# A fused two-layer transformer kernel on one core: five more landing places for expert weights, first weight parts run on the first 128 tokens, query rests moved to VectorE

## The reference, cut to what matters

```python
def peer_ffn(h, w_q, sub_keys, expert_u, expert_v):
    ...
        q = (hb @ w_q).reshape(PEER_TOKEN_BLOCK, PEER_HEADS, 2, PEER_HALF)
        s = jnp.einsum('thpc,hpkc->thpk', q, sub_keys).astype(jnp.float32)
        top_s, top_i = lax.top_k(s, PEER_TOPK)
        ...
        u = expert_u[idx]
        act = jax.nn.gelu(jnp.einsum('thkd,td->thk', u, hb).astype(jnp.float32), approximate=False)
        wts = (gates * act).astype(hb.dtype)
        return jnp.einsum('thk,thkd->td', wts, expert_v[idx])

def hybrid_layer(x, c, lb, rel_bias, ...):
    ...
    (aq, ak, av, iq, ik, iw, bq, bf, bi, bg, cq, ck, cv, cg, ga, gb, gc) = split_cols(h @ w_in)
    ...
    x = x + gt1 * (merged @ w_out)
    h2 = rmsnorm_2(x, norm2_g) * (1.0 + sc2) + sh2
    x = x + gt2 * hier_moe(h2, rg_w, rg_b, re_w, re_b, e_gate, e_up, e_down)
    return x
```

## Time and profile before

| | us |
|---|---|
| median of 3 runs (lowest, highest) | 2014.12 (2011.47, 2016.54) |
| the profiled execution, its own time | 2012.58 |
| its span in the trace | 2010.8 |

### The profile page before, as it was taken

One profiled execution on the slowest core, in us unless ns is written; L12 is line 12 of the kernel. 1 busy time (PEld: TensorE's weight loads), 2 busy tenths in 40 slices (PEclk: granted clock), 3 DMA queues, 4 the chain that ended last, 5 costly groups with the idle time before them and its releaser, 6 DMA issues.

```text
span 2010.8 us, 21920 instructions
## 1 busy us (share of the span) xinstructions
PE 1658.6 (82%) x8644; PEld 1020.0 (51%) x8644; DVE 988.1 (49%) x1894; ACT 547.6 (27%) x951; POOL 616.4 (31%) x396
## 2 busy tenths in 40 slices
PE   7998977677777777777999998999999867676765
PEld 7784942232222223236999988987884311111211
DVE  6462666876778775553663886554434100000001
ACT  4342421212222212123453544445622000000001
POOL 3431643444444444433674105443320000000000
PEclk9999998999999999998999999999999877778878
DMA  8755499999999999984544433554586999999997
GB/s 336 302 200 217 191 374 421 422 420 421 421 421 421 418 419 414 419 366 149 171 165 159 147 106 126 187 186 156 184 348 248 422 421 422 421 421 421 421 422 319
DMA packets 92228, 634.73 MB, mean 316 GB/s; under 512 B 10940, under 2 KB 13628, under 8 KB 16472
## 3 DMA queue, kind: packets, MB, share of 16 engines
q1 hardware_dynamic: 50832, 353.39, 45.1%
q0 software_dynamic: 36864, 268.45, 32.4%
q10 hardware_dynamic: 4424, 11.42, 1.6%
HBM read 632.15 MB, written 1.08 MB: 315 GB/s over the span
## 4 chain that ended last, share of the span: by engine, by line
PE 47%; DMA 42%; DVE 7%; ACT 2%; issue 2%; POOL 0%; SPq 0%; DVEq 0%; ACTq 0%
DMA t<-in_expert_uv,t 21%; PE ps L555 6%; PE ps L557 6%; PE ps L560 6%; DMA t<-in_eg 6%; DMA ring<-in_ed 5%; DMA t<-in_ed 5%; PE ps L596 3%; PE ps L755 3%; DMA ring<-in_eg 3%; PE ps L609 3%; PE ps L758 3%; DVE t L2018 3%; PE ps L575 2%; PE ps L576 2%; PE ps L581 2%
## 5 line engine op out<-in xcount | busy, mean ns | idle before, releaser
L179 POOL TENSOR_TENSOR t<-ring,t 128x1024 fp32r<-128x1024 f32 x125 | 320.8, 2576 | 474.7 <-ACT t L171 474.4
L755 PE MATMUL ps<-t 128*128 128x512 f32 x496 | 275.6, 638 | 163.3 <-ACT t L1384 163.2
L2685 POOL DMA_INDIRECT t<-in_expert_uv,t x248 | 280.9, 1133 | 360.3 <-PE ps L758 340.1
L2018 DVE CUSTOM_DVE_ANT_0 t<-t 128x1024 f32<-128x1024 f32 x248 | 303.0, 1226 | 171.9 <-DMA t<-in_expert_uv,t 169.4
L171 ACT ACTIVATE t<-ring 128x1024 fp32r<-128x1024 f32 x220 | 230.6, 1054 | 238.8 <-PE ps L560 87.2
L758 PE MATMUL ps<-t 128*128 128x512 f32 x496 | 260.0, 606 | 0.0
L755 PEld LDWEIGHTS ps<-t 128*128 128x128 f32 x496 | 87.3, 195 | 326.1 <-ACT t L1384 261.8
L1057 PE MATMUL ps<-t 128*32 128x512 f32 x864 | 144.5, 765 | 74.6 <-DMA t<-in_eg 28.0
L179 DVE TENSOR_TENSOR t<-ring,t 128x1024 fp32r<-128x1024 f32 x95 | 129.2, 1366 | 134.9 <-ACT t L171 132.1
L555 PE MATMUL ps<-t 128*128 128x256 f32 x1120 | 164.7, 291 | 15.1 <-ACT t L171 5.5
L1377 ACT ACTIVATE t<-t 128x2 f32<-128x2 f32 x129 | 26.2, 203 | 507.9 <-DVE t L2018 507.5
(11 more groups left out here) (358 smaller groups left out, 1841.5 us busy)
## 6 DMA issues: line engine op xcount, KB each, us to landing
ring<-in_w_in SPq DMA_DIRECT2D x82, 1024.0 KB, 5.0
t<-in_eu SPq DMA_DIRECT2D x38, 1024.0 KB, 26.9
t<-in_eg SPq DMA_DIRECT2D x36, 1024.0 KB, 26.9
t<-in_ed SPq DMA_DIRECT2D x34, 1024.0 KB, 27.3
ring<-in_ed SPq DMA_DIRECT2D x30, 1024.0 KB, 27.0
ring<-in_eg SPq DMA_DIRECT2D x28, 1024.0 KB, 26.8
ring<-in_eu SPq DMA_DIRECT2D x26, 1024.0 KB, 27.1
ring<-in_ada_w SPq DMA_DIRECT2D x20, 1024.0 KB, 7.5
```

The costliest lines, as they stand in the source:

```text
L179: e.tensor_tensor(p.lo, p.view, p.hi.bitcast(F32), ALU.subtract).then_inc(self.w.lo[eng], 1)
L755: ins = e.matmul(sums[tt][0], s.diag[col % 4], v[:, 1024:1536], start=first, stop=last)
L2018: ins = e.tensor_tensor_reduce(out=g[:, 0:1024], in0=g[:, 0:1024], in1=s.hN[:, col // 128, :], scale=1.0, scalar=0.0, op0=ALU.mult, op1=AL ...
L2685: m.gathered[s.place[col]].up(e.indirect_dma_start(out=s.gb[col], out_offset=None, in_=m.a_in["expert_uv"], in_offset=bass.IndirectOffsetO ...
```

## The change

**Expert places.** The ring `m.s4.w` has 18 places, and a 19th stands alone as `m.s4.w0` and holds the first `eg` chunk. The new ones are `more`, `g12` (rows 1 and 2 of `grow`, now in one tensor), `hT`, `x` and `selT`; `rw` and `cm` move into `sgb`. SP loads `more` and `selT` when the last `w_branch_c` matmul is done (`mc4`, 3, 3), now ahead of the two first ring buffers; then the ring as before; then `g12` after the last of four `h3` steps, `hT` after the router's matmuls (`route`), `x` after the matmuls that read it (`x_read`), and only then goes on with the places of `ada_w_2`. A branch for overfull experts (not taken with these inputs) turns the activations anew.

**First parts.** `pe_cols_begun` runs a part's 24 matmuls over the first 128 tokens as soon as tile 0 is there; `pe_cols` then does the other 128. It is used for 1 part in stage 1, 3 in stage 2 and 4 in stage 3.

**Rests.** Six of the 13 `w_q` rests of GpSimd (p7, p8, p9, p11, p13, p15) go to VectorE, put between steps of its picks; and all four rests of stage 3's first parts are made before `finish(1)`, where two were.

```diff
@@ lay_out
-        s.sp.expect(pair(a["w_q"], n), ("G", "G", "GGVG", "VGVG")[n], "cols")
+        s.sp.expect(pair(a["w_q"], n), ("G", "GGGV", "V", "V")[n], "cols")
...
-    early, then = cqk + rest, oct_
-    o.w = Weights(early + then + last, sem, "_e")
+    early, then = cqk + rest, oct_ + [more]
+    o.w = Weights(early + then + last + [m.g12, hT, x_t[:, :]], sem, "_e", False)
+    o.w0 = Weights([selT], sem, "_f", False)
...
+def pe_part(e, sp, p, o, xs, cols):
+
+    xh, xl = xs
+    for k in range(8):
+        e.matmul(o, p.hi[:, k, :], xh[:, k, cols], start=k == 0, stop=False)
+    for k in range(8):
+        e.matmul(o, p.hi[:, k, :], xl[:, k, cols], start=False, stop=False)
+    sp.rest(e, p)
+    for k in range(8):
+        ins = e.matmul(o, p.lo[:, k, :], xh[:, k, cols], start=False, stop=k == 7)
+    return ins
+def pe_cols_begun(m, e, sp, key, xs, n):
+
+    begun = []
+    for i in range(n):
+        if i % 2 == 0:
+            ps = m.b.claim(e, sub(key, i // 2))
+        p = sp.take(e, "pe")
+        pe_part(e, sp, p, ps[:, i % 2 * 256:i % 2 * 256 + 128], xs, slice(0, 128))
+        begun.append((ps, p))
+    return begun
...
+            if i < len(begun):
+                ps, p = begun[i]
+                ins = pe_part(e, sp, p, ps[:, j * 256 + 128:j * 256 + 256], xs, slice(128, 256))
...
@@ pe_retrieval
+    e.wait_ge(*b.taken(("hT2", 0, 1)))
+    begun = pe_cols_begun(m, e, s.sp, ("q", 0), s.hT, 3)
     pe_turn_tile(m, e, "hT2", s.hN[:, 1, :], 1, m.normed)
-    e.wait_ge(*b.taken(("hT2", 0, 1)))
...
+    e.wait_ge(*b.taken(("hT3", 0, 1)))
+    m.begun = pe_cols_begun(m, e, m.s3.sp, ("iq", 0), m.s3.hT, 4)
@@ dve_retrieval
-    run(dve_picks(m, e, 0, 0, (0,)))
+    picks = dve_picks(m, e, 0, 0, (0,))
+    pour(picks, 10)
+    s.sp.lows(e, "V", s.q0 + 8)
+    pour(picks, 7)
+    s.sp.lows(e, "V", s.q0 + 9)
+    run(picks)
...
-    m.s3.sp.lows(e, "V", 2)
+    m.s3.sp.lows(e, "V", 4)
@@ sync_program
+    e.wait_ge(*b.full(("mc4", 3, 3)))
+    load(e, we, 8, 9)
+    load(e, m.s4.w0, 0, 1)
     for n in range(RING):
         released(e, w, w.chunks[len(w.chunks) - RING + n])
-        load(e, we, 8 + n, 9 + n)
-    load(e, we, 8 + RING, 196)
+        load(e, we, 9 + n, 10 + n)
+    at = 9 + RING
+    e.wait_ge(m.h3.sem, 4)
+    load(e, we, at, at + 1)
+    e.wait_ge(*b.full("route"))
+    load(e, we, at + 1, at + 2)
+    e.wait_ge(*b.full("x_read"))
+    load(e, we, at + 2, at + 3)
+    load(e, we, at + 3, 195)
```

More of the change, by code:

```diff
@@ L280, in lay_out @@
     x_t = sb("x", 2048)
-    m.grow = [sb(f"g{i}", 1024)[:, :] for i in range(4)]
+    g03, m.g12 = (sb(f"g{i}", 2048)[:, :] for i in range(2))
+    m.grow = [t[:, i * 1024:i * 1024 + 1024] for t, i in ((g03, 0), (m.g12, 0), (m.g12, 1), (g03, 1))]
     m.cid = sb("cid", 144)
@@ L543, in pe_turn_tile, with pe_cols @@
         m.b.told(ins, (key, tt, kq))
-def pe_cols(m, e, sp, key, xs):
+def pe_part(e, sp, p, o, xs, cols):
     xh, xl = xs
+    for k in range(8):
[15 more added lines that the diff above has]
+    return begun
+def pe_cols(m, e, sp, key, xs, begun=()):
     for half in range(2):
-        ps = m.b.claim(e, sub(key, half))
+        if 2 * half >= len(begun):
+            ps = m.b.claim(e, sub(key, half))
         for j in range(2):
[L552 to L560, removed]
+            i = 2 * half + j
+            if i < len(begun):
+                ps, p = begun[i]
+                ins = pe_part(e, sp, p, ps[:, j * 256 + 128:j * 256 + 256], xs, slice(128, 256))
+            else:
+                p = sp.take(e, "pe")
+                ins = pe_part(e, sp, p, ps[:, j * 256:j * 256 + 256], xs, slice(0, 256))
             sp.through[p.n] = m.b.told(ins, sub(key, half))
@@ L763, in pe_retrieval @@
     for n in range(4):
-        for part, _ in enumerate(pe_cols(m, e, s.sp, ("q", n), s.hT)):
+        for part, _ in enumerate(pe_cols(m, e, s.sp, ("q", n), s.hT, begun if n == 0 else ())):
             p = 4 * n + part
@@ L781, in pe_retrieval @@
             pe_turn_tile(m, e, "hT3", s.hN[:, 0, :], 0, m.finished)
-    b.usable = list(range(8))
+    e.wait_ge(*b.taken(("hT3", 0, 1)))
+    m.begun = pe_cols_begun(m, e, m.s3.sp, ("iq", 0), m.s3.hT, 4)
+    held = [b.at["iq", 0, n][0] for n in range(2)]
+    b.usable, b.next = [i for i in range(8) if i not in held] + held, 0
 def run(steps):
@@ L1039, in pe_routing @@
         for n in range(2):
-            e.matmul(m.sums[tt][n], m.ident, m.x[:, tt, n * 512:n * 512 + 512], start=True, stop=False)
+            ins = e.matmul(m.sums[tt][n], m.ident, m.x[:, tt, n * 512:n * 512 + 512], start=True, stop=False)
+    b.told(ins, "x_read")
     b.usable, b.next = [0, 1, 2, 3], 3
@@ L1052, in pe_four @@
 def pe_four(m, e, key, ps, lhs, chunk, j0, first, last):
-    w = r3(chunk.ap, 4)
-    e.wait_ge(*m.s4.w.ready(chunk))
+    w, of = r3(chunk.ap, 4), m.s4.w0 if chunk in m.s4.w0.chunks else m.s4.w
+    e.wait_ge(*of.ready(chunk))
     for j in range(4):
@@ L1058, in pe_four @@
                        start=first, stop=last)
-    m.s4.w.through[chunk.n] = m.b.told(ins, key)
+    of.through[chunk.n] = m.b.told(ins, key)
 def pe_experts(m, e):
@@ L1146, in pe_dense @@
     o, b = m.s4, m.b
+    for tt in range(2):
+        for kq in range(2):
+            ps = b.claim(e, ("hT5", tt, kq))
+            for j in range(4):
+                k = 4 * kq + j
+                ins = e.transpose(ps[:, j * 128:j * 128 + 128], r3(m.hold, 2)[:, tt, k * 128:k * 128 + 128], m.ident)
+            b.told(ins, ("hT5", tt, kq))
+    for tt in range(2):
+        for kq in range(2):
+            e.wait_ge(*b.taken(("hT5", tt, kq)))
     for ex in range(32):
@@ L2075, in dve_retrieval @@
     weighted(1)
+    s.sp.lows(e, "V", s.q0 + 16)
     dots(2)
@@ L2600, in dve_dense @@
     tmp = o.xg[0].rearrange("p a b -> p (a b)")[:, 0:512]
+    for tt in range(2):
+        for kq in range(2):
+            dve_out(m, e, ("hT5", tt, kq), o.selT[:, 4 * kq:4 * kq + 4, tt * 128:tt * 128 + 128], 4)
     e.wait_ge(*b.full(("xg", 7, 1)))
```

60 lines of the change are left out of this document (32 added, 28 removed).

## The result

The changed kernel is slower: 2027.13 us, median of 7 runs (2018.36 to 2032.21), against 2014.62 for the kernel before (7 runs, 2011.47 to 2018.42). The ratio is 1.006, 95% interval 1.0042 to 1.0078. The forecast was 2007.2, 0.3% faster, with a range up to 2016: the sign was wrong, and the time lies outside the range.

The account below looks back on a forecast made before the run. Bound by transfers in two stretches (414 to 422 GB/s), elsewhere paced by PE. Terms 0 + 0.7 + 0 + 0.9 - 8.5 = -6.9 us took the median from 2014.12 to 2007.2; own range 2002.5 to 2012, with rivals 2000 to 2016.

Parts of the forecast that it names:

- the sign: Whole kernel: faster by 6.9 us, about 0.3%; chance 0.60 of faster by over 0.3%, 0.04 of slower by over 0.3%.
- So the cold start is gone: Stage 2, three begun parts: the half-speed start (2.5 us) vanishes, doubled weight loads eat that and more, +0.7 us.
- the bounds (0.060 to 0.120 us a matmul): Begun halves, matmul of 128 tokens: 0.060 if moved columns alone counted, 0.120 if it costs what the whole does.
- The price of a half part: Begun parts: 0.112 us per 128-token matmul, so a part in two halves costs 5.4 us where the whole cost 2.9.
- Stage 3's sum: Stage 3, four begun parts: second halves end at 935.25 where p4 began at 934.34, +0.9 us (-5 to +2.4).
- Stage 1: Stage 1, one begun part: second half ends at 20.5 to 22.5 against 21.5, taken as 0 (-1 to +1 us).
- The rests on VectorE: Stage 2's first pick: first gather at about 228 in place of 230.14, hidden because the 13th waits for PE; cost 0.
- the rival on the slow side: Stage 2: PE waits for the six rests moved to VectorE, each late, 13.6 us in all, 2020.8; chance 0.06.
- The places: Five expert places: the 23rd chunk lands at 1557.3 in place of 1565.8, -8.5 us (bounds -5.0 to -12.4).
- cheap halves: Rival, stages 1 to 3: a matmul of 128 tokens costs 0.060 us, giving 1992.4; chance 0.10.
- the early pick: Rival, stage 2: the earlier first pick moves the gather stream by -2 in place of +0.7, giving 2004.5; chance 0.08.
- the places gave most of their time: Rival judged here: the places give nothing, PE holds the experts' stream, the 8.5 us fall away, 2015.7; chance 0.06.

Follow-up runs that it names:

- Halves, filled: Changed kernel with eight overwritten 512-column matmuls behind the second tile's turn in stages 2 and 3: 2011.39 us, ratio 0.9985 to the kernel before.
- filled, whole: Changed kernel without begun parts, with overwritten matmuls in TensorE's pauses in stages 1 to 4 and the routing: 1999.74 us, ratio 0.9922 to the kernel before.
- no halves: Changed kernel with no part begun in any stage and stage 3's rests as before: 2007.32 us, ratio 0.9968 to the kernel before.
- halves alone: Kernel before with only the begun halves added (1, 3 and 4 parts): 2034.01 us, ratio 1.0095 to the kernel before.

## Why the prediction was wrong, point by point

Some starts, from the traces (us). "Halves, filled" is the first profile of the wide filling, "filled, whole" the fastest kernel. The medians come from different groups of runs; the kernel before had 2013.65 to 2016.11 beside them.

| | before | after | no halves | halves alone | halves, filled | filled, whole |
|---|---|---|---|---|---|---|
| stage 2, turn of tile 0 | 189.78 | 192.07 | 189.67 | 192.10 | 192.22 | 188.61 |
| first scores | 212.21 | 220.89 | 211.95 | 220.13 | 215.43 | 208.70 |
| second scores | 218.86 | 229.97 | 218.60 | 228.46 | 222.13 | 215.34 |
| last column's second half | 910.64 | 922.04 | 911.89 | 920.78 | 913.82 | 907.97 |
| stage 3, eight parts done | 947.77 | 969.54 | 949.71 | 966.62 | 950.06 | 943.47 |
| turn at the last projection | 1524.35 | 1544.72 | 1524.89 | 1545.16 | 1525.21 | 1517.95 |
| median | 2014.62 | 2027.13 | 2007.32 | 2034.01 | 2011.39 | 1999.74 |

Between "after" and "no halves" the lag is 2.4 at the first row, 11.4 at the third, 10.2 at the fourth, 19.8 at the fifth and 19.8 at the sixth, and the medians differ by 19.8. Stages 2 and 3 cost 9 to 10 us each, and all of it reaches the end.

**The step that failed** is "So the cold start is gone" in stage 2, and its twin in stage 3. The sum itself contained a pause: 0.45 + 2.23 us from the turn to the second half. It was costed as time and not as a cause. Before the change a pause of 4 us and then one of 1.57 dropped the clock, and whole parts brought it back after some 7 us; I took the first pause for the only cause and held that, with it filled, nothing falls. And the bounds (0.060 to 0.120 us a matmul) left out the price at the half clock, although the prediction took 0.17 to 0.21 for the half of stage 1; 0.213 is what the runs show (eight matmuls in 1.71). With it, the second halves from 209.5 on are 5.6 us longer (six groups by 0.81, the one before them by 0.7), the first scores 0.9, p3 1.6, and the weight loads 0.8: 8.9, where 11.4 - 2.4 = 9.0 were measured. A rival, that the clock falls in the halves and stays down, was missing, and it was the case that decided.

**The price of a half part** was right: 0.112 us (0.893 for a group of 8). With the clock kept full, stage 2's first scores stood 215.43 - 192.22 = 23.2 us behind the turn of tile 0, against 22.4 before: +0.8, forecast +0.7.

**Stage 3's sum had a misread row.** It let p4 begin at 934.34; that row is the second group of p3. The row that was wanted, from the same timeline of the kernel before:

```profile
936.26 1.12 PE L555 MATMUL ps<-t 128*128 128x256 f32 x8
```

p4 began at 936.26. Rightly counted the term was -1.0, not +0.9, and that is what the filled run gives: 938.50 - 913.82 = 24.7 from the last column to p4, against 25.6.

**Stage 1**, forecast 0 (-1 to +1): the trace has 2.4, outside these bounds. The prediction had the clock risen by the end of the second half (20.5 to 22.5); it rose at 28.2, behind both halves. How much of it is in the median stays open, as one program alone moved by 3.

**The rests on VectorE**: right. First gather 2.9 us earlier (forecast 2), 13th unmoved, no change of time shown. No rest was late; the rival on the slow side named the wrong engine.

**The places**: right in mechanism, -6.6 in place of -8.5. The interval (4.4 to 9.5 us) holds both. In that run's trace the projection's end stood 0.8 later, at 1525.14 in place of 1524.35.

**The rivals**: cheap halves fell (0.112), the early pick did not carry through, the places gave most of their time, and VectorE was not late. The only rival that made the kernel slower (2020.8) rested on late rests, not on the clock.

## What to carry to other kernels

Before work is split into narrower pieces to start earlier, look at where TensorE pauses within and behind it: a fall of the clock that whole parts repaired in 6 us left these halves at the half clock until whole parts returned (14 to 24 us). Not every narrow stream did that here, so look at the granted clock in a trace of the split work before the split is kept. Price a new stream at both clocks, and make "the clock falls in it" a rival whenever the sum has a pause in it. Where a wait can't be removed, matmuls whose result is overwritten, sized to end before the wait does, keep the clock: with parts whole and the places kept they brought the time to 0.9922 of that before (0.9968 without fillers), while the split with the same places had 1.006.

## What the runs showed of the hardware

- Of two steady streams of the same halves, unbroken in both cases, one stayed at 0.213 us for 41 us and the other at 0.112 us for 43 us. They were entered at different clocks.
- Other 128-column streams did bring the clock back: L1108 at 1550.8 in the run without halves, and the turns at 13.3 in the second profile of the filled kernel. What separates them from the halves is not shown.
- At the starts of stages 2 and 3 the fall followed a pause: 1.75 us between halves in four places of two kernels, 2.75 between whole parts in one, 4.00 and 7.79 ahead of the turns in the kernel before. With the 1.75 us filled by wide or by narrow matmuls it did not happen, in six places of three profiles. The length of one pause does not settle it alone: 1.57 us between whole parts passed, and L1108 lost the clock behind 1.27 and 1.00.
- When the clock first rises differs from run to run of one program: it rose at 13.3 us in one profile and at 28.8 in another, and stage 2 began 3 us apart. The kernel after spreads over 14 us in 7 runs, the one before over 7; no profile here tells what makes that difference.
